# Gathering expert results after the last expert's weights, and an earlier silu-times-up product on VectorE

## The chip, the cores and the metric

The kernel runs on one core of a Trainium2 chip. The metric is the device time of one execution in microseconds (us); the kernel before took 1556.19 us, the median of three runs (1555.83 to 1558.44).

## What is computed

Two blocks on 512 tokens of width 1024, in float32. The first is two attention layers, and the second an attention and convolution layer followed by a mixture of experts and a last norm. Only the mixture and the last norm matter here:

```python
y_e = (silu(x_e @ w_gate[e]) * (x_e @ w_up[e])) @ w_down[e]   # for each of 32 experts, on its own rows
out[token] = x[token] + sum over the token's two experts of weight * y_e[row]   # gate folded in
out = rms_norm(out, g_final)
```

Each token picks two of the 32 experts. An expert has three weight matrices of 2048 KB each (gate, up, down), so the mixture streams 32 x 3 of them from memory.

## The kernel before, in words

The program is written by hand, one instruction stream for each engine, tied by semaphores. What an engine runs is in the order of its stream; nothing overtakes.

The mixture is a list of 32 items, one expert each, ordered by how many rows the expert has. SyncE issues the three weight loads of an item (`load_expert`, L602 to L610) into one of three sets of buffers (`it.p`), each when the item three places earlier has read its matrix; arrival is counted on `e_in[p][0..2]` (gate, up, down). All go through one queue, q1.

An item on TensorE (`item`, L1242) is: gate and up products (`gate_up`, L1191), then, when VectorE has multiplied silu(gate) by up (`swiglu`, L2462 to L2468), four or fewer transposes (L1263), and when ScalarE has copied these back (L1646), the down product (`down`, L1218). VectorE scales the result by the norm gate (`gated_results`, L2470 to L2484), and ScalarE stores it to the buffer `ys` in memory (`expert_results`, L1653), for all items but the last two.

The results of the first 30 items are brought to their tokens by GpSimd: it waits for every such store (`y_out`, L1767 and L1768), then issues eight indirect DMAs (L1772), two for each of the four token tiles `t`, of 128 rows of 4 KB each. `gath[t]` counts them. VectorE adds both to `x` in `add_results(t)` (L2498 to L2504).

The last two items (30 and 31), with few rows, aren't stored. TensorE multiplies their results by a selection matrix (`sums`, L1231 to L1240, with the matmuls of `sum_up` at L1227), eight banks for each item, and VectorE adds each bank to `x` (`add_sum`, L2492 to L2496). `sums(0)` stands ahead of item 31 on TensorE, `sums(1)` is its last work. After the experts each engine reads a word that says whether some expert had more rows than planned (L1280, L1659, L1775, L2551) and branches past a loop; here it has none to run. VectorE then makes the additions of `sums(1)`, ScalarE the squares of the last norm (L1665), GpSimd the reciprocal root (`rstd`, L1682 to L1692), VectorE the last product (L2572), and SyncE stores `out` (L651).

So the end of VectorE's stream before is: additions of `sums(0)`; `add_results(0)` and `(1)`; the product of silu and up for item 31; `add_results(2)` and `(3)`; the gated result of item 31; the read and branch; the additions of `sums(1)`.

Of the kernel before, what the change touches and what calls it, by code (L numbers as in the profile page):

```python
# [161 lines left out]
def fused_kernel(nc, a, out, xs, ys, table):  # L162

    with ExitStack() as ctx:
# [3 lines left out]
        def sem(name):  # L168
            return ctx.enter_context(nc.semaphore(name))
# [208 lines left out]
        e_in = [[sem(f"expert_{n}_loaded{p}") for n in ("gate", "up", "down")] for p in range(3)]  # L378
# [148 lines left out]
        items = plan.items  # L527
# [29 lines left out]
        def bank_of_sum(j):  # L557


            return psum[2 * (1 + j % 3) + late_pieces[0].bank] if j < SUMS else psum[j % 4]  # L560
# [1108 lines left out]
        def _(pool):  # L1669
# [97 lines left out]
            for n in range(5):  # L1767
                pool.wait_ge(y_out[n], 16 * (P // (NARROW if n > 2 else WIDE)) * plan.stores[n])  # L1768
            pool.sem_inc(pool_passed, 1)
            for t in range(TT):  # L1770
                for k in range(2):
                    gp.indirect_dma_start(gathered[k][:, t, :], None, ys[:, :],  # L1772
                                          bass.IndirectOffsetOnAxis(ap=dest[:, k, t:t + 1], axis=0)).then_inc(gath[t], 16)
# [13 lines left out]
        def _(dve):  # L1787
# [5 lines left out]
            def chain(ins):  # L1793
                steps(ins)
                steps.settle()
# [666 lines left out]
            def swiglu(it, unrolled=True):  # L2462
                for pc in it.pieces:
                    if not unrolled or pc.used:
                        dve.wait_ge(hT_done[pc.bank], pc.used)
                    dve.wait_ge(sg_ready[pc.bank], pc.used + 1)
                    v.tensor_tensor(h_act[pc.bank][:, 0:pc.ff], sg[pc.bank][:, 0:pc.ff], psum[2 + pc.bank][:, pc.ff:2 * pc.ff],  # L2467
                                    ALU.mult).then_inc(h_ready[pc.bank], 1)  # L2468

            def gated_results(it, unrolled=True):  # L2470


                for pc in it.pieces:
                    dve.wait_ge(down_done[pc.bank], pc.used + 1)
                    if unrolled and pc.stores:
                        dve.wait_ge(y_out[pc.buffer], 16 * pc.tiles_stored * pc.stores)
                    if pc.slots is None or pc.size == WIDE:
                        v.tensor_tensor(y_buf[pc.buffer][:, 0:pc.cols], psum[6 + pc.bank][:, 0:pc.cols], gates[pc.size], ALU.mult)\
                            .then_inc(y_ready[pc.bank], 1)
                        continue  # L2480
                    times = W // pc.cols
                    v.tensor_tensor(y_buf[pc.buffer].rearrange("p (c n) -> p c n", c=times),
                                    psum[6 + pc.bank][:, 0:pc.cols].unsqueeze(1).to_broadcast([P, times, pc.cols]),
                                    late_gate.rearrange("p (c n) -> p c n", c=times), ALU.mult).then_inc(y_ready[pc.bank], 1)  # L2484
# [7 lines left out]
            def add_sum(j, bank, done, taken, n):  # L2492

                t, cols = place_of_sum(j)
                dve.wait_ge(done, n + 1)
                v.tensor_tensor(x[:, t, cols], bank[:, :], x[:, t, cols], ALU.add).then_inc(taken, 1)  # L2496

            def add_results(t):  # L2498

                dve.wait_ge(gath[t], 32)  # L2500
                for k in range(2):
                    chain(v.scalar_tensor_tensor(out=x[:, t, :], in0=gathered[k][:, t, :], scalar=own_slot[:, k * TT + t, 3:4],
                                                 in1=x[:, t, :], op0=ALU.mult, op1=ALU.add))
                dve.sem_inc(results_added, 1)  # L2504
# [37 lines left out]
            for j in range(SUMS):  # L2542
                add_sum(j, bank_of_sum(j), summed_up, sum_taken, j)
            dve.wait_ge(sum_taken, SUMS)
            add_results(0)
            add_results(1)
            swiglu(items[-1])
            add_results(2)
            add_results(3)
            gated_results(items[-1])  # L2550
            n_pairs = dve.value_load(over_ids[0:1, OVER + 1:OVER + 2], min_val=0, max_val=OVER // 2)  # L2551
            with dve.If(n_pairs > 0):
                flip(further_items(0)[0], items[-1])
# [96 lines left out]
```

## Time and profile before

| | us |
|---|---|
| three runs | 1556.19 median, 1555.83 to 1558.44 |
| span of the profiled execution | 1554.6 |
| around that span, taken as the median less the span | 1.5 |
| TensorE busy | 1383.2 (89%) |
| VectorE busy | 698.1 (45%) |
| ScalarE busy | 356.0 (23%) |
| GpSimd busy | 112.0 (7%) |

The profile is of one execution. All times in it count from the start of its span. The change touches only the last 60 us of it, so the views of that stretch say what it is worth: the chain of work that ended last, the timelines of the engines, and the DMA queues. q1 holds the weight loads and the store of `out`, q10 the stores of expert results, q0 what GpSimd issues (the gathers, and before them the rows of each item), and q8 and q14 instructions. A "q" behind an engine's name marks work of its sequencer (waits, reads of a word, branches, DMA issues).

### The profile page before, as it was taken

What the parts mean: (1) busy time and instruction counts of PE and PEld (TensorE: products, weight loads), DVE (VectorE), ACT (ScalarE), POOL (GpSimd) and SP (SyncE); (2) the same over time, 40 slices, a digit from 0 to 9 for tenths busy, and PEclk for the clock granted to TensorE, in tenths of its full rate; (3) what the DMA queues carried; (4) which work ended last, traced back from release to release, by engine and by line L of the source; (5) the groups of instructions that cost most, each with busy time, mean ns of one, the idle gap of its engine ahead of it and who ended that gap; (6) DMA issues with size and microseconds to landing.
All of it is one profiled execution on the core that took longest, in us unless ns stands there. A gap on an engine that the chain in (4) does not pass through costs nothing.

```text
span 1554.6 us, 17575 instructions
## 1 busy us (share of the span) xinstructions
PE 1383.2 (89%) x6694; PEld 699.9 (45%) x6694; DVE 698.1 (45%) x1274; ACT 356.0 (23%) x778; POOL 112.0 (7%) x227
## 2 busy tenths in 40 slices
PE   4999999999999999999899978979996977869784
PEld 2444445554464445664644445455442333323341
DVE  4675515884366623322499775263121112111125
ACT  2433205562310344421400064110000000000001
POOL 3000000100100000002100000112000000000012
PEclk9999999999999999999899999989997989889996
DMA  9763136004376541003524123169999999999994
GB/s 340 268 243 109 54 108 129 1 1 162 100 259 211 188 162 55 1 0 109 165 81 161 54 109 151 66 247 391 421 416 418 422 419 416 425 420 426 421 401 168
DMA packets 85133, 338.08 MB, mean 217 GB/s; under 512 B 10343, under 2 KB 16280, under 8 KB 72376
## 3 DMA queue, kind: packets, MB, share of 16 engines
q1 hardware_dynamic: 70752, 307.24, 50.8%
q0 software_dynamic: 5664, 13.70, 3.1%
q10 hardware_dynamic: 8632, 15.99, 2.9%
q8 instruction: 55, 0.90, 0.2%
q14 instruction: 30, 0.25, 0.0%
HBM read 323.34 MB, written 17.24 MB: 219 GB/s over the span
## 4 chain that ended last, share of the span: by engine, by line
PE 68%; DMA 15%; DVE 11%; issue 3%; ACT 2%; POOL 1%; DVEq 0%; SPq 0%; ACTq 0%; POOLq 0%
PE score_banks L712 14%; PE bank L720 13%; DMA slots<-in_w_exp_up 11%; PE score_banks L1191 9%; PE bank L1218 5%; PE score_banks L720 4%; PE bank L928 3%; PE bank L696 3%; PE score_banks L1205 2%; PE bank L883 2%; PE bank L1030 2%; PE score_banks L1021 2%; DVE bufD L1982 2%; PE score_banks L940 1%; DMA slots<-in_w_mod 1%
## 5 line engine op out<-in xcount | busy, mean ns | idle before, releaser
L712 PE MATMUL score_banks<-slots 128*128 128x512 f32 (+1 forms) x584 | 246.0, 579 | 6.2 <-ACTq L1350 3.6
L720 PE MATMUL bank<-slots 128*128 128x512 f32 x480 | 209.4, 593 | 2.0 <-PE bank L720 0.9
L1191 PE MATMUL score_banks<-slots,norm_row 128*64 128x512 f32 (+1 forms) x672 | 151.5, 617 | 44.3 <-DMA slots<-in_w_exp_up 42.0
L712 PEld LDWEIGHTS score_banks<-slots 128*128 128x128 f32 x584 | 112.5, 195 | 132.9 <-issue 129.5
L2467 DVE TENSOR_TENSOR mix<-probsT,score_banks 128x256 f32<-128x256 f32 (+1 forms) x39 | 14.4, 370 | 285.3 <-ACT probsT L1641 285.1
L720 PEld LDWEIGHTS bank<-slots 128*128 128x128 f32 x480 | 89.9, 190 | 112.9 <-issue 111.7
L1218 PE MATMUL bank<-slots,mix 128*64 128x512 f32 (+1 forms) x864 | 118.3, 489 | 11.5 <-issue 9.5
L1641 ACT ACTIVATE probsT<-score_banks 128x256 f32<-128x256 f32 (+1 forms) x39 | 13.4, 343 | 441.7 <-PE score_banks L1191 381.2
L1191 PEld LDWEIGHTS score_banks<-slots,norm_row 128*64 128x64 f32 (+1 forms) x672 | 50.6, 144 | 139.1 <-issue 137.8
L720 PE MATMUL score_banks<-slots 128*128 128x512 f32 (+1 forms) x256 | 95.2, 527 | 0.3 <-PE score_banks L720 0.3
L2359 DVE SCALAR_TENSOR_TENSOR bufD<-slots,col,bufD 128x512 f32<-128x512 f32 x120 | 80.5, 750 | 0.4
L1218 PEld LDWEIGHTS bank<-slots,mix 128*64 128x64 f32 (+1 forms) x864 | 45.8, 124 | 68.1 <-issue 61.3
L1191 PE MATMUL score_banks<-slots,mix 128*32 128x256 f32 x896 | 57.2, 412 | 21.1 <-DMA slots<-in_w_exp_up 21.1
L1982 DVE SCALAR_TENSOR_TENSOR bufD<-slots,silu_c,bufD 128x512 f32<-128x512 f32 x91 | 68.4, 752 | 5.0 <-DMA slots<-in_w_mod 1.6
L2060 DVE TENSOR_TENSOR mix<-bank,gate_row 128x512 f32<-128x512 f32 x24 | 16.6, 692 | 112.9 <-PE bank L720 112.6
L720 PEld LDWEIGHTS score_banks<-slots 128*128 128x128 f32 x256 | 46.4, 190 | 44.1 <-issue 44.1
L928 PE MATMUL bank<-slots 128*128 128x512 f32 x128 | 61.8, 613 | 0.4 <-PE bank L883 0.4
L1682 POOL TENSOR_SCALAR pw<-ss 128x1 f32<-128x1 f32 (+3 forms) x25 | 7.1, 284 | 764.3 <-ACT slots L1338 411.9
L1736 POOL DMA_INDIRECT bufD<-normed_rows,w_router x30 | 30.5, 1016 | 411.1 <-PE score_banks L1180 387.0
L696 PE MATMUL bank<-k_sb,slots 128*128 128x128 f32 x312 | 45.4, 284 | 14.8 <-DVE slots L2425 9.4
L1982 DVE SCALAR_TENSOR_TENSOR slots<-slots,silu_c 128x512 f32<-128x512 f32 x70 | 52.6, 752 | 9.2 <-DMA slots<-in_w_mod 6.3
L1191 PEld LDWEIGHTS score_banks<-slots,mix 128*32 128x32 f32 x896 | 32.7, 118 | 50.6 <-issue 37.6
(358 smaller groups left out, 1722.8 us busy)
## 6 DMA issues: line engine op xcount, KB each, us to landing
slots<-in_w_exp_down SPq DMA_DIRECT2D x32, 2048.0 KB
slots<-in_w_exp_gate SPq DMA_DIRECT2D x32, 2048.0 KB, 28.8
slots<-in_w_exp_up SPq DMA_DIRECT2D x32, 2048.0 KB, 33.6
slots<-in_w_in SPq DMA_DIRECT2D x16, 2048.0 KB, 8.8
slots<-in_w_mod SPq DMA_DIRECT2D x24, 1024.0 KB, 5.2
slots<-in_ada_w SPq DMA_DIRECT2D x18, 1024.0 KB, 6.7
slots<-in_w_out SPq DMA_DIRECT2D x6, 2048.0 KB, 7.8
slots<-in_ada_w SPq DMA_DIRECT2D x3, 2048.0 KB, 20.3
```

The costliest lines, as they stand in the source:

```text
L696: last = nc.tensor.transpose(bank[:, i * P:(i + 1) * P], piece, ident)
L712: last = mm(bank[:, cols], w[:, k, lo:lo + P], src[:, k, cols], start=(k == 0), stop=(k == kts - 1))
L720: last = mm(bank[:, 0:cols], src[:, k, t * P:(t + 1) * P], rhs(k), start=(k == 0), stop=(k == kts - 1))
L883: last = mm(psum[banks][r][:, :], rows[:, k, r * P:(r + 1) * P], weights[:, k, :], start=(k == 0), stop=(k == 3))
L928: ins = mm(gate_bank(group)[:, :], hT[:, k, t * P:(t + 1) * P], z_units[u][:, k, :], start=(k == 0), stop=(k == KT - 1))
L1021: mm(bank[:, :], hT[:, 2 * pair + c, t * P:(t + 1) * P], A8[:, 2 * pair + c, :], start=True, stop=False)
L1030: last = mm(bank[:, c * P:(c + 1) * P], pT[:, j * P:(j + 1) * P], C_tok[:, j, h * P:(h + 1) * P], start=(j == 0), stop=(j == TT - 1))
L1191: last = mm(out, rows[:, k, :], e_gu[it.p][:, :, k, c * pc.ff:(c + 1) * pc.ff], start=(k == 0), stop=(k == KT - 1))
L1205: last = mm(psum[2 + pc.bank][c * pc.size:(c + 1) * pc.size, m * pc.ff:(m + 1) * pc.ff], rows[:, k, :], e_gu[it.p][:, m, k, c * pc.ff:(c + ...
L1218: last = mm(psum[6 + pc.bank][c * pc.size:(c + 1) * pc.size, 0:pc.cols], hTe[pc.bank][:, lo:lo + pc.size], e_down[it.p][:, f, c * pc.cols: ...
L1982: return v.scalar_tensor_tensor(out=acc, in0=w, scalar=c, in1=acc, op0=ALU.mult, op1=ALU.add)
L2359: conv_at[j] = steps(v.scalar_tensor_tensor(out=conv[:, j, :], in0=src, scalar=wcol, in1=conv[:, j, :], op0=ALU.mult, op1=ALU.add))
```

## The change

GpSimd waits, ahead of its eight gathers, for the down weights of the last item. VectorE makes the last item's product of silu and up ahead of `add_results(0)`, and its gated result between `add_results(1)` and `(2)`.

```diff
@@ gpsimd, L1767 @@
             for n in range(5):
                 pool.wait_ge(y_out[n], 16 * (P // (NARROW if n > 2 else WIDE)) * plan.stores[n])
             pool.sem_inc(pool_passed, 1)
+            pool.wait_ge(e_in[items[-1].p][2], 16 * items[-1].loads)
             for t in range(TT):
                 for k in range(2):
                     gp.indirect_dma_start(gathered[k][:, t, :], None, ys[:, :],
@@ vector, L2542 @@
             for j in range(SUMS):
                 add_sum(j, bank_of_sum(j), summed_up, sum_taken, j)
             dve.wait_ge(sum_taken, SUMS)
+            swiglu(items[-1])
             add_results(0)
             add_results(1)
-            swiglu(items[-1])
+            gated_results(items[-1])
             add_results(2)
             add_results(3)
-            gated_results(items[-1])
             n_pairs = dve.value_load(over_ids[0:1, OVER + 1:OVER + 2], min_val=0, max_val=OVER // 2)
```

## Rows read from the trace of the kernel before

**Rows 1.** The page: TensorE clock, DMA busy share and rate in 40 slices.
```profile
PEclk9999999999999999999899999989997989889996
DMA  9763136004376541003524123169999999999994
GB/s 340 268 243 109 54 108 129 1 1 162 100 259 211 188 162 55 1 0 109 165 81 161 54 109 151 66 247 391 421 416 418 422 419 416 425 420 426 421 401 168
```

**Rows 2.** The chain that ended last: start us, us, what.
```profile
1499.66 10.68 DMA expert_results<-bufD
...
1510.36 0.02 POOLq L1768
...
1510.64 0.76 issue
1511.40 0.97 POOL slots L1772
...
1515.16 11.47 DMA slots<-expert_results,dest
...
1530.72 3.64 PE bank L1218 x32
1534.36 1.70 issue
```

**Rows 3.** Timeline of VectorE: start us, us, engine, line, operation, count, idle before.
```profile
1523.82 2.60 DVE L2502 SCALAR_TENSOR_TENSOR x<-slots,sums,x 128x1024 f32<-128x1024 f32 x2 [6.70 <-DMA slots<-expert_results,dest]
...
1529.69 5.35 DVE L2502 SCALAR_TENSOR_TENSOR x<-slots,sums,x 128x1024 f32<-128x1024 f32 x4
1535.27 0.69 DVE L2482 TENSOR_TENSOR bufD<-bank,slots 128x512 f32<-128x512 f32 x1 [0.22 <-DVE x L2502]
1538.14 1.29 DVE L2496 TENSOR_TENSOR x<-score_banks,x 128x512 f32<-128x512 f32 x2 [2.18 <-PE score_banks L1227]
1539.85 4.16 DVE L2496 TENSOR_TENSOR x<-score_banks,x 128x512 f32<-128x512 f32 x6 [0.42 <-PE score_banks L1227]
```

**Rows 4.** Timeline of SyncE: the issues of item 31's gate and down weights.
```profile
1482.49 0.34 SPq L610 DMA_DIRECT2D slots<-in_w_exp_gate  x1
...
1485.81 0.33 SPq L610 DMA_DIRECT2D slots<-in_w_exp_down  x1
```

**Rows 5.** DMA issues from 1482.4 to 1483.5: KB each, us to landing.
```profile
slots<-in_w_exp_gate SPq DMA_DIRECT2D x1, 2048.0 KB, 28.8
```

**Rows 6.** DMA queues in 1510:1512, 1518:1520, 1520:1522, 1522:1524: packets, MB, share.
```profile
q1 hardware_dynamic: 38, 0.52, 61.3%
...
q1 hardware_dynamic: 18, 0.23, 26.9%
...
q1 hardware_dynamic: 4, 0.03, 3.9%
...
q0 software_dynamic: 216, 0.80, 98.3%
```

**Rows 7.** Stretches: busy us (count) by engine, granted clock, DMA share, GB/s.
```profile
1490.00:1495.00 5.00, 4.08 (x26) 1.72 (x24) 1.25 (x4) 0.77 (x2) 0.00 (x0) 1.00 1.01 426
...
1526.00:1528.00 2.00, 0.00 (x0) 0.00 (x0) 1.72 (x3) 0.00 (x0) 0.00 (x0) 0.50 0.45 184
1528.00:1530.00 2.00, 0.17 (x1) 0.17 (x1) 1.78 (x3) 0.00 (x0) 0.00 (x0) 0.50 0.25 102
```

**Rows 8.** Timeline of GpSimd: the first two and the last of the eight gathers.
```profile
1511.40 0.97 POOL L1772 DMA_INDIRECT slots<-expert_results,dest  x1 [26.17 <-issue]
1512.67 0.95 POOL L1772 DMA_INDIRECT slots<-expert_results,dest  x1 [0.30 <-issue]
...
1520.14 0.94 POOL L1772 DMA_INDIRECT slots<-expert_results,dest  x1 [0.30 <-issue]
```

**Rows 9.** Line 1772, all eight gathers, from issue to landing.
```profile
DMA to landing us min/median/max: 6.9/9.2/11.5
```

**Rows 10.** DMA issues, whole span: the store of the output.
```profile
out<-slots SPq DMA_DIRECT2D x4, 512.0 KB, 2.7
```

**Rows 11.** Line 2551 on VectorE's sequencer: ns min/median/max.
```profile
L2551 DVEq TENSOR_LOAD <-inv_sums x1: 546/546/546, 1535.3 to 1535.3; - x1
```

**Rows 12.** Timeline of TensorE and ScalarE: item 31's gate and up, its silu.
```profile
1516.62 2.86 PE L1191 MATMUL score_banks<-slots,norm_row 128*32 128x256 f32 x44 [0.24 <-issue]
...
1524.47 0.28 ACT L1641 ACTIVATE probsT<-score_banks 128x128 f32<-128x128 f32 x1 [16.51 <-PE score_banks L1191]
```

## The prediction

> **What bounds the kernel now.** I read the page's 40 slices first. From the slice at about 1050 us on, the DMA engines are full and move some 420 GB/s until the last two slices [rows 1]: the mixture runs at the rate of its weights. The change doesn't touch that rate. It touches what comes after the weights, so the next view is the chain of work that ended last. It goes from the last store of expert results, which lands 10.68 us after its issue, to GpSimd's wait at 1510.36, to the gathers, and stays with a gather until 1526.64 [rows 2]. From there VectorE adds the gathered rows and makes item 31's product, TensorE multiplies by the down weights (3.64 us) and sums, and VectorE adds the sums.
>
> The timeline of VectorE shows how tight this end is. It has nothing from 1517 until the first pair of gathers is in at 1523.8, then four `add_results` with little idle time up to 1535.04 (5.35 us from 1529.69), the gated result until 1535.96, then 2.18 us idle while TensorE sums, and the eight additions from 1538.14 to 1544.01 [rows 3]. What follows is the norm and the output store, which the change leaves as they are. So the number to forecast is when the last addition ends, now 1544.01.
>
> Last, the DMA queues. The down weights of item 31 are issued at 1485.81, behind gate and up [rows 4]. Gate, issued at 1482.49, lands 28.8 us later [rows 5], at 1511.3. q1 still moves 0.52 MB in 1510 to 1512, 0.23 MB in 1518 to 1520 and 0.03 MB in 1520 to 1522 [rows 6]. The last weights are thus in at about 1521 to 1522, 10 us after GpSimd began to gather. While gathers and weights run together the DMA share isn't full at first (q1 61.3% in 1510 to 1512, when hardly a gather moves yet), and at the end it falls to 0.45 and 0.25 with gathers left [rows 6, 7]. The 16 engines reach their ends at different times: some have had their weights long before, and those that had weights until 1521 finish the gathers last.
>
> **The change, part by part.** *GpSimd's new wait.* It lets the gathers start only when the down weights are in. I need that time without gathers beside it. From 1511.3 two loads of 2.097 MB (up and down) are left for the engine that is last; at the 426 GB/s of the full stretch [rows 7] one takes 4.92 us, so 1521.2. Gate and up and down share the engines with gathers now, and some of those 9.9 us may shrink as other engines fall idle. The lower bound comes from q1's packets being large (0.52 MB in 38) and the gathers' small (0.80 MB in 216) [rows 6]: if both queues take turns by packet, 3.7 KB of gather stand beside 13.7 KB of weights, a fifth of the engine's time in 1513 to 1521.5, or 1.8 us, and the weights would be in at 1519.7 rather than 1521.5. I take 1520.8, near the row of the full stretch, with 1519.7 and 1521.8 as ends.
>
> Behind the waiting instruction on GpSimd's queue stand the eight gathers, its own read and branch, and the reciprocal roots of the last norm, which wait for VectorE's last additions in any case. From the last wait to the first gather it takes 1.04 us (1510.36 to 1511.40, 0.76 us of it preparation) [rows 2]; three of the waits that are now in it are then past, so I take 0.95. A gather is issued every 1.25 us (1511.40 and 1512.67, 1520.14 for the eighth) [rows 8]. First issue 1521.75, second 1523.0, eighth 1530.5.
>
> *How long a gather takes with no weights beside it* is what the trace doesn't show. Eight of them took 6.9 to 11.5 us to landing, all in a crowd [rows 9]; that is the upper side. The lower side is 0.94 us in which GpSimd writes the descriptors [rows 8] and the 2.7 us that a 512 KB store of `out` takes on idle engines [rows 10]: 3.6 us. The second waits up to 1.25 us for the first, which is as large. I take 4.5, nearer to the idle case because nothing else is queued. So the first pair is in at 1527.5 (now 1523.8), the last at 1535.0 by the issues, and hardly sooner by the bytes: 4.19 MB at 410 GB/s are 10.2 us.
>
> The Trainium skill gives this price in DMA: Bandwidth & Descriptors, "Anatomy of one DMA": 2.0 us and the bytes at 436 GB/s, an estimate of 3.2 us for 512 KB, or 4.1 with the writing of descriptors. No run here shows it. By it, the end would come some 0.4 to 1.3 us sooner than with my 4.5.
>
> *VectorE's order.* `add_results` costs 2.75 us to the next one (1529.69 to 1535.04 is two of them, 5.35) [rows 3], so four are 10.95 us with their waits, and the gated result between them adds 0.69 and about 0.1. From 1527.6 that is 11.7 us: 1539.3. The last pair of gathers, in at 1535.0, would allow an end at 1537.7, so the adding is the bound, by 1.6 us. Item 31's product of silu and up is moved ahead of it all. Its cover: silu is done at 1524.75 now, and gate and up begin at 1516.62 [rows 12]; both are before 1527.5, so the product (0.29 us), the transposes, the copy and the down product (3.64 us at the clock of 0.50 that rows 7 show) end before 1530, beside VectorE's wait and additions. That takes item 31's product and down product off the chain. The gated result then has its input when its turn comes, at about 1533.2, and TensorE's first four sums (3.8 us) are ready at about 1538, before VectorE wants them.
>
> *What this uncovers.* Now the gated result is VectorE's last work ahead of the branch, and the read of the word and the branch lie in the 2.18 us in which it waits for the sums. After the change they stand open behind `add_results(3)`. The read is 0.55 us [rows 11], with the register work and the branch 0.97 us from 1535.29 to 1536.26; what the first instruction past the branch costs isn't seen. Bounds: 1.0 us, and the 2.85 us from 1535.29 to 1538.14, at which the sums came in. I take 1.6. So the eight additions start at 1540.9. Six of them take 4.16 us back to back [rows 3], eight 5.6. TensorE refills a bank in 0.95 us at the low clock while VectorE takes 0.7, and with four filled ahead that still is enough.
>
> *Sum.* 1520.8 + 0.95 + 1.25 + 4.5 + 0.1 + 11.7 + 1.6 + 5.6 = 1546.5, against 1544.01: 2.5 us later. Of it, the start of the first pair is 3.7 later, the chain of VectorE behind it from the first gather to the last addition is 18.9 us against 20.2 now. To the median, 1556.2 + 2.5 = 1558.7.
>
> **The rivals.**
> 1. *The wait is longer than it seems (slower).* The pair lands as in a crowd: all 16 engines gather at once from one memory, no longer some early and some late. At the row's least, 6.9 us [rows 9], the end is 2.4 us later than in the sum: +4.9, 1561.1. With weights at 1521.8 as well, +5.9, 1562.1. It decides from 5.1 us on, where the total loss passes 3.1 us. For it: each of the eight rows. Against it: the engines were loaded in all of them.
> 2. *The reordering is worth more than the delay.* Weights at 1519.7, a pair in 3.6 us, 1.0 for the branch: 2.6 us less than the sum, so -0.1, 1556.1. To be faster by over 3.1 us, even with these low ends, the weights would have to be in at 1516.7, when at the full rate the up weights alone are due (1511.3 + 4.9 = 1516.2); this takes engines that speed up greatly once others are idle.
> 3. *The wait doesn't bind.* If, in most executions, the down weights are in before the stores, only the new order counts. VectorE ends `add_results(3)` at 1535.1 or up to 0.5 later for the gated result between, reads and branches by 1537.2, and ends at 1542.8: -1.2, 1555.0. q1's bytes until 1522 speak against it [rows 6].
>
> The Trainium skill, DMA: Bandwidth & Descriptors, "Queues, rings and completion order", says that each DMA engine takes its queues in turn, a packet at a time. Here the 128 KB store beside the weights took 10.68 us, in agreement with a shared engine. The rule speaks for the change as far as the weights go, and it is the lower end of 1519.7 above; it doesn't turn the sign, since the gathers' bytes must be moved behind the weights all the same.
>
> **How the numbers follow.** About 0.2% (3.1 us) is what a measurement of this kernel can tell from no change. The forecast, a loss of 0 to 3.1 us: 0.50. Rival 1, with other ways to lose more: 0.35. Rival 2: 0.08, a third of it faster by over 0.2%. Rival 3: 0.05, all within 0.2%. Faster by something that isn't in the trace: 0.02. So faster 0.05, same 0.60, slower 0.35. The range from 1555.0 (rival 3) to 1562.1 (rival 1 at its upper end) leaves out 2 in 10. Most of the cases inside are above the time before, so a loss that can hardly be measured is what I expect.
>
> **What would show it.** In the changed kernel's profile, GpSimd's first gather at 1521 to 1523 and none before the last weights; DMA nearly idle for 2 to 3 us between them; landings within 5 us of issue; VectorE's first gathered addition at 1527 to 1528; the down product of item 31 well before that; and the eight additions starting 1.0 to 2.0 us after `add_results(3)` with no idle time between. I am wrong if the weights are in before 1519 or after 1523, if gathers land under 3.6 us or over 6, or if the branch shows no cost.

## The result and the profile after

The changed kernel took 1562.31 us (median of 8 runs, 1559.62 to 1565.85) against 1557.3 us for the kernel before (8 runs, 1555.54 to 1558.44): the ratio is 1.0036, with an interval from 1.0027 to 1.0045. It is slower by 5.0 us in the medians (5.6 by the ratio), more than the 3.1 us that were called the limit of what can be told. A second comparison gave 1.0025 (1.0011 to 1.0039).

The profiled execution has a span of 1559.7 us, 5.1 more than before. First the timeline of GpSimd in the changed kernel (start us, us, engine, line, operation, idle time before it), which answers to [rows 8]:

```profile
1523.24 0.96 POOL L1773 DMA_INDIRECT slots<-expert_results,dest  x1 [36.78 <-DMA slots<-in_w_exp_down]
1524.51 0.95 POOL L1773 DMA_INDIRECT slots<-expert_results,dest  x1 [0.31 <-issue]
...
1532.71 1.01 POOL L1773 DMA_INDIRECT slots<-expert_results,dest  x1 [0.30 <-issue]
```

The gathers wait for the down weights, and start 11.8 us later than before. The stretches of the same kernel (busy us of TensorE, its weight load, VectorE, ScalarE and GpSimd, then granted clock, DMA share, GB/s) show what that leaves on the DMA engines:

```profile
1510.00:1512.00 2.00, 1.92 (x32) 1.08 (x32) 0.08 (x2) 0.00 (x0) 0.00 (x0) 1.00 0.65 279
...
1518.00:1520.00 2.00, 1.96 (x33) 1.26 (x36) 1.04 (x2) 0.00 (x0) 0.00 (x0) 1.00 0.23 98
1520.00:1522.00 2.00, 2.00 (x40) 1.13 (x31) 0.00 (x0) 0.00 (x0) 0.00 (x0) 1.00 0.11 41
1522.00:1524.00 2.00, 0.78 (x13) 0.48 (x13) 0.29 (x1) 0.56 (x2) 0.76 (x1) 1.00 0.00 0
1524.00:1526.00 2.00, 1.50 (x28) 0.78 (x20) 0.00 (x0) 0.00 (x0) 1.39 (x3) 1.00 0.40 66
1526.00:1528.00 2.00, 0.00 (x0) 0.00 (x0) 0.00 (x0) 0.00 (x0) 1.64 (x2) 1.00 0.98 385
```

In 1510 to 1512 the share of busy DMA engines has begun to fall. In 1518 to 1522 the DMA share is 0.23 and 0.11: most of the 16 DMA engines have had their weights and stand still, where in the kernel before they gathered. From 1522 to about 1525 all of them stand still. Then VectorE's timeline, which answers to [rows 3]:

```profile
1522.49 0.29 DVE L2468 TENSOR_TENSOR mix<-probsT,score_banks 128x128 f32<-128x128 f32 x1 [3.44 <-ACT probsT L1641]
1530.31 5.35 DVE L2503 SCALAR_TENSOR_TENSOR x<-slots,sums,x 128x1024 f32<-128x1024 f32 x4 [7.53 <-DMA slots<-expert_results,dest]
1535.88 0.69 DVE L2483 TENSOR_TENSOR bufD<-bank,slots 128x512 f32<-128x512 f32 x1 [0.22 <-DVE x L2503]
1536.49 5.35 DVE L2503 SCALAR_TENSOR_TENSOR x<-slots,sums,x 128x1024 f32<-128x1024 f32 x4
1543.46 4.15 DVE L2497 TENSOR_TENSOR x<-score_banks,x 128x512 f32<-128x512 f32 x6 [1.62 <-issue]
1547.91 1.29 DVE L2497 TENSOR_TENSOR x<-score_banks,x 128x512 f32<-128x512 f32 x2 [0.30 <-PE score_banks L1227]
```

The product of silu and up is out of the way, VectorE waits 7.53 us for the first pair of gathers, and from 1530.31 on it hardly stops until the last addition ends at 1549.20, 5.2 us later than 1544.01. The branch stands open with 1.62 us. The down product of item 31, which before ran at 1530.72 in 3.64 us at a granted clock of 0.50 (1.2 GHz) [rows 2, 7], follows the gate and up products closely and takes 1.93 us, at 1.00 (2.4 GHz):

```profile
1518.36 3.66 PE L1191 MATMUL score_banks<-slots,norm_row 128*32 128x256 f32 x64
1522.83 0.33 PE L1263 MATMUL bank<-k_sb,mix 128*128 128x128 f32 x1 [0.81 <-DVE mix L2468]
1523.57 1.93 PE L1218 MATMUL bank<-slots,mix 128*32 128x256 f32 x32 [0.41 <-issue]
1536.67 3.78 PE L1227 MATMUL score_banks<-bufD,sinT 64*128 64x512 f32 x8 [11.17 <-DVE bufD L2483]
```

That gain is real and lies beside VectorE's wait, where it is worth nothing.

### The profile page after: what moved, and what is told of

Its sections match the earlier page's. It is cut to its first block, busy times and chain, and to the rows that moved or that the text cites. A ratio compares the mean times of both kernels' runs of the same rounds, so it can differ in the third digit from the quotient of the medians.

```text
span 1559.7 us, 17574 instructions
## 1 busy us (share of the span) xinstructions
PE 1380.8 (89%) x6694; PEld 703.8 (45%) x6694; DVE 698.3 (45%) x1274; ACT 356.2 (23%) x778; POOL 112.3 (7%) x227
## 4 chain that ended last, share of the span: by engine, by line
PE 63%; DMA 17%; DVE 14%; issue 3%; ACT 2%; POOL 1%; SPq 0%; DVEq 0%; POOLq 0%; ACTq 0%
DMA slots<-in_w_exp_up 13%; PE bank L720 12%; PE score_banks L712 10%; PE score_banks L1191 8%; DVE bufD L2360 5%; PE score_banks L720 5%; PE bank L1218 4%; PE bank L696 3%; PE bank L928 3%; PE score_banks L1205 2%; PE bank L883 2%; PE bank L1030 2%; PE score_banks L1021 2%; DMA slots<-in_ada_w 2%; DVE bufD L1983 2%
## 5 line engine op out<-in xcount | busy, mean ns | idle before, releaser
L1191 PE MATMUL score_banks<-slots,mix 128*32 128x256 f32 x896 | 54.6, 399 | 19.3 <-DMA slots<-in_w_exp_up 19.3
L696 PEld LDWEIGHTS bank<-k_sb,slots 128*128 128x128 f32 x312 | 35.8, 147 | 38.8 <-DVE slots L2426 16.8
## 6 DMA issues: line engine op xcount, KB each, us to landing
slots<-in_w_exp_down SPq DMA_DIRECT2D x32, 2048.0 KB, 36.3
slots<-in_w_exp_gate SPq DMA_DIRECT2D x32, 2048.0 KB, 29.5
slots<-in_ada_w SPq DMA_DIRECT2D x3, 2048.0 KB, 20.5
```

The lines of the kernel that those rows point to most:

```text
L696: last = nc.tensor.transpose(bank[:, i * P:(i + 1) * P], piece, ident)
L1191: last = mm(out, rows[:, k, :], e_gu[it.p][:, :, k, c * pc.ff:(c + 1) * pc.ff], start=(k == 0), stop=(k == KT - 1))
```

## The experiments

Three theories were set against each other. *A:* the loss is the late start of the gathers. *B:* VectorE's new order costs it (the insertion between the additions, and the open branch). *C:* the weight stream of the changed program is itself later, and little of the loss is the wait's.

**How the profiles are compared.** The mixture before the end doesn't take the same time in each execution. So I count from one event, G: the landing of item 31's gate weights on the last of the DMA engines. It is the issue in SyncE's timeline and the time to landing in the DMA issues. In the kernel before 1482.49 + 28.8 = 1511.3 [rows 4, 5]; in the changed one 1483.73 + 29.5 = 1513.2, and its down weights are in at 1487.04 + 35.9 = 1522.9:

```profile
1483.73 0.34 SPq L610 DMA_DIRECT2D slots<-in_w_exp_gate  x1
1487.04 0.33 SPq L610 DMA_DIRECT2D slots<-in_w_exp_down  x1
slots<-in_w_exp_gate SPq DMA_DIRECT2D x1, 2048.0 KB, 29.5
slots<-in_w_exp_down SPq DMA_DIRECT2D x1, 2048.0 KB, 35.9
```

All columns but G are us after G, good to 0.1. The pair is in when VectorE's first addition of it starts. The last pair's landing is the last issue and its time to landing; that of the down weights their issue and theirs, which the first profile of before doesn't give (q1 has one packet, of 0.00 MB, left in 1522 to 1524 there).

| kernel | G | first gather | down weights | first pair | last pair | last addition |
|---|---|---|---|---|---|---|
| before | 1511.3 | 0.1 | | 12.5 | 20.3 | 32.7 |
| before, again | 1512.2 | 0.5 | 12.2 | 13.6 | 21.0 | 32.5 |
| new order, no wait | 1514.2 | -0.5 | 11.4 | 12.4 | 19.8 | 31.3 |
| spread order, no wait | 1512.0 | 0.7 | 11.1 | 13.1 | 20.6 | 31.6 |
| waits for up | 1513.1 | 5.1 | 9.9 | 12.3 | 20.5 | 31.3 |
| waits for up, early read | 1509.9 | 5.1 | 9.9 | 13.0 | 20.5 | 31.4 |
| the same, again | 1514.2 | 5.1 | 10.0 | 12.3 | 21.0 | 30.8 |
| the change | 1513.2 | 10.0 | 9.7 | 17.1 | 24.9 | 36.0 |
| the change, again | 1510.5 | 10.1 | 9.8 | 17.0 | 25.0 | 36.3 |
| wait alone, old order | 1511.8 | 10.0 | 9.7 | 16.5 | 25.3 | 37.4 |

**The new order alone.** In the changed kernel:

```diff
-            pool.wait_ge(e_in[items[-1].p][2], 16 * items[-1].loads)
```

> The new order on VectorE alone, GpSimd's gathers start as in the kernel before. Theory A (the loss of 5 us is the gathers' late start): between -0.6 and +0.5 us against the kernel before. VectorE waits for silu until 1524.75 instead of starting on gathered rows at 1523.8 (+1.0), has the gated result in between (+0.5), opens the branch (+1.6), and loses the 2.2 us of waiting for the sums. Theory B (the new order costs it): +3 us or more. Theory C (the changed program's weight stream is itself some 2 us later): about +2 us, with the last stores landing near 1512 instead of 1510.4.

Measured: 1557.03 us (12 runs), ratio 1.0003 (0.9994 to 1.0011). B falls. In time the order neither costs nor gives anything that shows; after G it is even 1.3 us shorter than before (31.3 against 32.6, the mean of the two profiles of before), since its TensorE work is ready in time. Its timeline of VectorE has both effects in it, 1.62 us at the branch and no wait for the down product:

```profile
1525.52 0.29 DVE L2467 TENSOR_TENSOR mix<-probsT,score_banks 128x128 f32<-128x128 f32 x1 [7.19 <-ACT probsT L1641]
1526.66 5.36 DVE L2502 SCALAR_TENSOR_TENSOR x<-slots,sums,x 128x1024 f32<-128x1024 f32 x4 [0.85 <-DMA slots<-expert_results,dest]
...
1539.81 4.16 DVE L2496 TENSOR_TENSOR x<-score_banks,x 128x512 f32<-128x512 f32 x6 [1.62 <-issue]
```

**The wait alone.** In the kernel before:

```diff
             pool.sem_inc(pool_passed, 1)
+            pool.wait_ge(e_in[items[-1].p][2], 16 * items[-1].loads)
```

> GpSimd's wait for the down weights alone, with VectorE's old order. Theory A: slower than the changed kernel by 1 us, so +6 us against before: the first two additions end at 1535.7 as in the changed kernel, then product, transposes, copy and down product end at about 1541, gated result 1542, first sum 1544.3, last addition 1550.2. Theory B: about +2 us. Theory C: +2 us more than what the gathers' start says, in both.

Measured: 1562.7 us (6 runs), ratio 1.0045 (1.0031 to 1.0059), +7.0 us by the ratio and 5.5 in the medians. The whole loss is in the wait, and after G the new order wins back 1 us or so of it: last addition at G + 37.4, against 36.0 and 36.3. The times of the two kernels can't be told apart, their intervals overlap.

**A wait for the up weights.** In the changed kernel:

```diff
-            pool.wait_ge(e_in[items[-1].p][2], 16 * items[-1].loads)
+            pool.wait_ge(e_in[items[-1].p][1], 16 * items[-1].loads)
```

> The changed kernel, but GpSimd waits for the last item's up weights instead of its down weights, which land 4.9 us earlier (1518.1 against 1523.0 in the changed kernel). Theory A, if each us of delay counts in full: +0 to +1 us against before. If instead the DMA engine that is last with its weights sets the end of the gathers, the gathers end only when that engine has done its down weights and 10 us of gathers: the gain over the changed kernel is then about 3 us, the empty time of that engine, so +2 us. Theory B: as slow as the changed kernel, +5 us.

Measured: 1555.68 us (12 runs), ratio 0.9993 (0.9983 to 1.0003). This run says most. GpSimd's first gather in it:

```profile
1518.24 0.96 POOL L1773 DMA_INDIRECT slots<-expert_results,dest  x1 [30.28 <-DMA slots<-in_w_exp_up]
```

and VectorE's first additions of gathered rows:

```profile
1525.39 5.36 DVE L2503 SCALAR_TENSOR_TENSOR x<-slots,sums,x 128x1024 f32<-128x1024 f32 x4 [2.75 <-DMA slots<-expert_results,dest]
```

The first gather is issued at 1518.24, that is G + 5.1, 5 us later than without a wait, and still the first pair is in at G + 12.3 and the last at G + 20.5, as without it (12.4 to 13.6, and 19.8 to 21.0). With the wait for down the issues are 4.9 us later again, and the pairs 4.7 and 4.4 us later. So a start at G + 5 is still free, and from there to G + 10 each us costs close to one. No start between the two was run; since a us of delay can't cost much more than one, nearly all of the 4.9 us must count, and the turn lies close to G + 5. The second of my expectations under A, that such a start would still cost 2 us, was wrong. Without a wait, what lands the gathers is the DMA engine that is last with its weights, whenever they were issued. The profile doesn't name single engines; that few are left at the end is read from the DMA share, 0.45 and then 0.25 in the kernel before [rows 7]. An estimate agrees: from G on, at 426 GB/s [rows 7], that engine has its share of two loads to move (9.8 us) and its share of eight gathers (4.19 MB, 9.8 us), which makes the first pair G + 12.3 and the last G + 19.7 at the earliest. Measured with starts up to G + 5.1 are 12.3 to 13.6 and 19.8 to 21.0. With the start at G + 5.1, GpSimd's issues reach G + 14.7, the last pair is in 5.9 us later, and the two limits meet. With the start at G + 10 the issues and the time to landing are the limit alone.

**Before and after, again.** Both kernels unchanged.

> The kernel before, unchanged, as a control of the comparison and for a second profiled execution. Counted from the landing of the last item's gate weights on the slowest DMA engine (G), the first profile had the first pair of gathers in at G + 12.4, the last at G + 20.3 and the last addition at G + 32.7 us. Theory A, in the form that the first runs leave (gathers may start up to about 5 us after G at no cost, and each us beyond costs one): the same three figures within 1 us, and 0 us in the comparison. Theory C: G itself lies within 1 us of the first profile's 1511.3. If G moves by 1 to 3 us between executions of one kernel, the 1.9 us of the changed kernel are chance and C falls.

> The changed kernel, unchanged, again beside the kernel before. Theory A: first gather issued at G + 10.0, first pair in at G + 17, last at G + 25, last addition at G + 36, so 3 to 4 us behind the kernel before in these terms, and +3 to +5.6 us in time. Theory C: G at 1513 or later again, and the time stays 2 us above what the last addition's distance from G gives.

Measured: before against before 1.0001 (0.9992 to 1.001), the change 1.0025 (1.0011 to 1.0039), +3.9 us. After G the figures of the changed kernel repeat within 0.3 us. Those of before repeat less well: last addition 32.7 and 32.5, but first pair 12.5 and 13.6, last pair 20.3 and 21.0. G itself doesn't repeat: 1510.5 here for the changed kernel, 1513.2 in the first profile, and 1509.9 to 1514.2 over all ten, with no order by kernel. C falls as the reason of those 1.9 us: the first profile of the change was behind at G by chance, and of the 5.1 us between the two spans some 3.3 are the change. What the time still has above that is taken up under the prediction.

**Another order without a wait.** In the kernel before:

```diff
             add_results(0)
-            add_results(1)
             swiglu(items[-1])
+            add_results(1)
             add_results(2)
-            add_results(3)
             gated_results(items[-1])
             n_pairs = dve.value_load(...)
+            add_results(3)
```

> No wait. VectorE makes the product of silu and up between add_results 0 and 1, the gated result between 2 and 3, and reads the word for the branch ahead of add_results 3. Theory A: faster than before by 1.0 to 2.0 us: the down product (3.6 us at the low clock) ends at 1531.7, the gated result at 1533.3, add_results 3 at 1536.1, the branch at 1536.8 and the eight additions at 1542.5, against 1544.0. Theory B: no gain or a loss, since each insertion delays the gathered additions. Theory C says nothing on it.

Measured: 1555.83 us (12 runs), ratio 0.9997 (0.9987 to 1.0008). After G the last addition is 1.0 us sooner than before, the low end of what was expected, and the time can't tell it from none.

**An early read.** In the kernel that waits for up:

```diff
             gated_results(items[-1])
+            n_pairs = dve.value_load(...)
             add_results(2)
             add_results(3)
-            n_pairs = dve.value_load(...)
```

> GpSimd waits for the last item's up weights, VectorE has the changed order, and the read of the word for the branch stands behind the gated result, ahead of add_results 2. Theory A: the read (0.9 us open behind add_results 3 in the changed kernel) lies beside the gated result; idle time between add_results 3 and the additions 0.7 instead of 1.62 us, and 0.9 us less than with the up wait alone, so 1.0 to 2.5 us faster than before. Theory B: no difference from the kernel with the up wait.

> The kernel with the up wait and the read ahead of add_results 2, a second time, to narrow the interval of its first comparison (0.9994, from 0.9985 to 1.0003). Theory A: the last addition at G + 30.5 to 31.5, against G + 32.5 to 32.7 in the two profiles of the kernel before, so 1 to 2 us or 0.06 to 0.13% faster than before.

Measured: 1553.73 us (11 runs), ratio 0.9994 (0.9985 to 1.0003), and in the second comparison 1556.26 us (12 runs), 0.9991 (0.9982 to 1.0000). VectorE's timeline in the second:

```profile
1533.02 5.36 DVE L2503 SCALAR_TENSOR_TENSOR x<-slots,sums,x 128x1024 f32<-128x1024 f32 x4 [0.23 <-issue]
1539.10 4.16 DVE L2497 TENSOR_TENSOR x<-score_banks,x 128x512 f32<-128x512 f32 x6 [0.73 <-DVE x L2503]
```

The gap at the branch is 0.73 us instead of 1.62, and 0.23 opens at the read: 0.7 us net. This is the best found of the kernels that give the right result. Both comparisons lean to a gain of about 1 us over the kernel before, and after G the last addition is 1.1 to 1.9 us sooner (31.4 and 30.8); it is under what one comparison can tell.

**Half the bytes.** The sum had 4.5 us from the second issue to the first pair, measured were 5.8 and 5.6 us. To see whether the bytes are the reason, each gather was cut to 64 rows, with the wait and, leaving its line out too, without it. The other 64 tokens of each tile get what was in the buffer.

```diff
-                    gp.indirect_dma_start(gathered[k][:, t, :], None, ys[:, :],
-                                          bass.IndirectOffsetOnAxis(ap=dest[:, k, t:t + 1], axis=0)).then_inc(gath[t], 16)
+                    gp.indirect_dma_start(gathered[k][0:64, t, :], None, ys[:, :],
+                                          bass.IndirectOffsetOnAxis(ap=dest[0:64, k, t:t + 1], axis=0)).then_inc(gath[t], 16)
```

> The changed kernel, but each gather brings 64 rows of 4 KB instead of 128; the other 64 tokens of each tile get what was in the buffer. Eight issues and the same waits stay, half the bytes go. In the changed kernel the first pair was in 5.8 us after the second issue, where 4.5 was forecast. If the bytes of both make up the difference: 4.2 to 4.6 us, first pair 1.4 us sooner, and the time 1.2 us or so less than the changed kernel's. If it is a fixed cost of such a DMA: 5.5 us or more, and no gain.

> The new order on VectorE without GpSimd's wait, and gathers of 64 rows instead of 128 (the other 64 tokens of each tile get what was in the buffer). Theory A says that without the wait the gathers end when the DMA engine that is last has moved its weights and then its share of gathered bytes: with half the bytes the last pair is in at about G + 15.5 to 17 instead of G + 20 to 21 (G: landing of the last item's gate weights), the first pair at G + 11 to 12. If instead GpSimd's issues set it, the last pair would stay 11 us behind the last issue. The down weights land at G + 10 to 10.8, between the 11.1 to 12.3 with full gathers beside them and the 9.8 with none. Time: 0 to 2.5 us under the kernel with the new order alone.

Measured: with the wait 1558.78 us (10 runs), ratio 1.0025 (1.0014 to 1.0036), first pair 5.2 us after the second issue. That is between the 4.2 to 4.6 and the 5.5 that would have decided, and the ratio is that of the changed kernel with full gathers: inconclusive. Without the wait 1568.62 us (4 runs), ratio 1.0066 (1.0051 to 1.0082), some 10 us slower than before with half the bytes, which none of the theories expected. Its stretches:

```profile
1515.00:1520.00 5.00, 2.04 (x7) 0.59 (x4) 2.75 (x5) 0.00 (x0) 3.61 (x4) 0.87 1.03 159
1520.00:1525.00 5.00, 0.00 (x0) 0.00 (x0) 0.00 (x0) 0.00 (x0) 1.80 (x2) 0.50 1.01 150
```

The DMA engines are busy throughout and move 150 GB/s, and the down weights land 50.9 us after their issue, where the kernels with full gathers and no wait have 36.1 to 36.7. So the edit had changed two things, the bytes and the partitions written. The next two keep all 128 partitions and halve the rows to 2 KB; they aren't the right halves, and the other half of each token's sum is what was in the buffer:

```diff
-                    gp.indirect_dma_start(gathered[k][:, t, :], None, ys[:, :],
+                    gp.indirect_dma_start(gathered[k][:, t, 0:W], None, ys.rearrange("r (h n) -> (r h) n", h=2),
```

> The changed kernel, but each gather brings 128 rows of 2 KB instead of 4 KB (halves of rows, not the right ones; the other half of each token's sum is what was in the buffer). The run with 64 rows changed a second thing: it wrote to half of the partitions, and moved 190 to 240 GB/s where the full gathers move 330 to 385. With all partitions in use and half the bytes, if bytes make up the difference to the forecast of 4.5 us: first pair in 4.6 us or less after the second issue (5.2 to 5.8 us with full rows), last pair 4.5 us or less after the last issue. If it is a fixed cost of such a DMA: 5.2 us or more for the first pair.

> The same gathers of 2 KB rows without GpSimd's wait, VectorE in the new order. The 64-row gathers beside the weights were 10 us slower, with the down weights in at G + 25 instead of G + 11.4 (G: landing of the last item's gate weights). If that came from writing to half of the partitions, the 2 KB rows don't show it: down weights in at G + 10 to 11, first pair at G + 11 to 12.5, last at G + 14 to 17 (the DMA engine that is last has half the gathered bytes left after its weights), and the time is at or up to 2.5 us under the kernel with the new order alone. If any gather of smaller pieces beside weights has this effect, the time is 5 us or more over it.

Measured with the wait (a single run, so the time says little): 1557.3 us against a median of 1557.28 for before. The time of the eight gathers from issue to landing is, in the changed kernel:

```profile
DMA to landing us min/median/max: 4.7/5.8/6.1
```

and in the kernel with half rows:

```profile
DMA to landing us min/median/max: 3.6/3.7/4.5
```

The first pair is in 4.5 us after the second issue. So the bytes make up the difference to the forecast, as far as one profile can say: 4.5 us is what a pair of half the size takes. The three profiles of full rows have 5.8, 5.6 and 5.2, so the step to the lowest of them, 0.7 us, is little more than their own spread. Without the wait: 1554.25 us (10 runs), ratio 0.9984 (0.9974 to 0.9994), down weights at G + 10.9, first pair at G + 11.1, last pair at G + 16.0, last addition at G + 30.1. The gathers' last landing moves 4 to 5 us forward with half of the 10 us of bytes, while GpSimd issues as ever: without a wait they are bound by the bytes of the last DMA engine, as A has it. The estimate above gives G + 11.1 and G + 14.8 for the two pairs here. The slow case didn't come back, so it isn't made by fewer bytes or smaller pieces. It goes with the form of 64 rows on 64 partitions; which of the two, the count of rows or the partitions, makes it wasn't separated.

## Why the prediction was wrong

The mechanism was right, and what was forecast as "no change that can be told" was a loss that can: 0.60 stood on within 0.2%, 0.35 on slower. The measured 1562.31 lies 0.2 us above the range. The signs listed came, later by the 1.9 us of G, but for the landings (4.7 to 6.1 us, not within 5) and what hangs on them, VectorE's first gathered addition at 1530.31. Term by term, in us after G of each profile (the forecast took G as 1511.3):

- *Weights in.* Forecast G + 9.5 (1520.8), measured 9.7 and 9.8. Two loads at the full rate, 1521.2 or G + 9.9, was the right estimate; I had gone below it for a gain from engines left alone, and none came. That gathers slow the weights is so: 11.1 to 12.2 in the three profiles without a wait that give it, 9.7 to 10.0 in the six with one. So the change does bring the weights 1.3 to 2.5 us sooner. The Trainium skill's rule that each DMA engine takes its queues in turn, a packet at a time (DMA: Bandwidth & Descriptors, "Queues, rings and completion order"), gave 1.8; by that rule, the traces agree on the difference. The forecast took it off the wrong figure: with gathers beside them the weights are in at G + 11.1 to 12.2 and not at G + 10.2 (1521.5), so the end 1519.7 was 1.3 us too low.
- *From the wait to the first gather.* Forecast 0.95, measured 0.2 to 0.3. The preparation of 0.76 us falls into the new wait. 0.7 too much.
- *The pair's time to landing.* Forecast 4.5, measured 5.8, 5.6, and 5.2 with the old order. This is the step that failed, a term mis-sized by 1.2 us. It was built from an idle store and one transfer ahead; the half-row run, with 4.5, suggests that the figure fits half the bytes. The Trainium skill's price for a gather (DMA: Bandwidth & Descriptors, "Anatomy of one DMA"), 3.2 us, is lower still: no gather of 512 KB landed under 4.6 us in the two profiles of the changed kernel, and half rows of 256 KB took 3.6 us at least where the page's sum gives 2.6. The 4.1 of the forecast puts GpSimd's 0.94 us on top, though the page counts the writing of descriptors in its 2.0. The measured times decide.
- *How times to landing are to be read.* Both gathers of a pair count on one semaphore, `gath[t]`, and the view takes the first half of the pair's arrivals for the first gather. So its figure for a first gather is only a lower bound, and that for a second is the pair's. In the second profile of before the eight alternate, 6.0 to 6.8 and 11.7. [rows 9] has figures for only two of its eight gathers, 6.9 and 11.5; the 6.9, on which the first rival was priced, is such a bound and no landing of a gather.
- *VectorE from the first pair to the last addition.* Forecast 18.9 (11.7, 1.6 and 5.6), measured 18.9 (1530.31 to 1549.20) in the first profile, with each part within 0.2, and 19.3 in the second, where VectorE waited 0.46 us for the second pair. The forecast had no wait there.
- *The kernel before.* Its last addition is at G + 32.7 and 32.5, as read.

Together: the forecast had the last addition at G + 35.2, the runs have it at 36.0 and 36.3; the loss by structure is 3.5 us where 2.5 were forecast. That alone puts it past the 3.1 us. Of the 3.6 us between the forecast time, 1558.7, and the measured 1562.3, this is 1.0. Another 1.1 is level: the three runs shown of before had a median of 1556.2, all eight 1557.3, and the forecast was built on the first. The other 1.5 stays open. Both comparisons show such a rest, of 2.1 and 0.4 us: they give +5.6 and +3.9 us, with intervals from 1.7 to 7.0 together, and the first one's lower end, 4.2, is above 3.5. The kernel with the wait alone shows it too (+7.0 by the ratio, 4.8 after G). No run says where it arises.

Of the rivals, the first (the pair lands late) was the case in kind, in part: its point of decision was put at 5.1 us, the landings took 5.2 to 5.8. Its reason, that all 16 engines gather at once, was tested by no run, and its other half, weights at 1521.8 (G + 10.5), didn't come. The second didn't occur: the DMA engine that is last didn't speed up when others fell idle. Two loads took 9.7 to 10.0 us after G in each kernel with a wait, against 9.84 at the rate of the full stretch. The third was excluded by GpSimd's idle row, which ends with the down weights. But its price, -1.2 us for the order alone, was about right after G (-1.3), though the time shows none of it.

One thing the prediction had no step for: the start of the gathers isn't what bound them before. It priced the delay from the landing (1523.8 to 1527.5) and got its size about right, but it didn't ask from which start on a delay begins to count. That point, close to G + 5, is what the wait for up shows.

## What to carry to other kernels

In this kernel, a transfer that shares the DMA engines with the last loads is bound by the engine that finishes those loads last. It can be issued later at no cost, up to the point where issue time and landing time alone reach that engine's end, and beyond it each us counts. So a wait that keeps two transfers apart is better set on an earlier load than the last. Here even that gave nothing that can be told in time (0.9993), since its gain (the weights, here 1.3 to 2.5 us sooner) is worth something only if those weights are what the end waits for. When profiles of single executions are compared for a few us, count from a common event near the end: here the stream ahead of it moved by 4.3 us between executions, more than the change did.

## What the runs showed of the hardware

- Gathers of 64 rows on 64 of 128 partitions, beside weight loads, held both up: 150 GB/s together with the DMA share at 1.0, and the last weights 14 us later. Half rows on all partitions, with the same bytes, didn't. Alone, the two forms can't be told apart by rate: 186 to 236 GB/s in 1524 to 1530 with the wait, and 168 to 221 in 1524 to 1532 for half rows. Both are near what GpSimd issues, 262 KB each 1.21 to 1.25 us, or 210 to 217 GB/s, so the 328 to 385 GB/s of full gathers, with twice the bytes for each issue, say nothing against them. The low rate named in the expectation for half rows is thus no sign of the partitions. From 1526 to 1528, with 64 rows and with half rows:

```profile
1526.00:1528.00 2.00, 0.00 (x0) 0.00 (x0) 1.44 (x2) 0.00 (x0) 1.54 (x2) 0.62 0.89 236
1526.00:1528.00 2.00, 0.00 (x0) 0.00 (x0) 1.74 (x2) 0.00 (x0) 1.70 (x2) 0.94 0.78 221
```

- The DMA engines' ends are far apart. In the changed kernel the DMA share falls to 0.65 in 1510 to 1512 already, with the last down weights in at 1523; the fast engines had theirs over 10 us before.
- Issuing a gather took longer once VectorE's additions ran. Before, all eight took 0.94 to 0.97 us; in the changed kernel the seventh, issued at 1530.73 just after VectorE had begun at 1530.31, took 1.67. Each full-gather kernel with a wait has one such gather, of 1.15 to 1.82 us. That VectorE is the reason is a reading of these times and was tested by no run:

```profile
1530.73 1.67 POOL L1773 DMA_INDIRECT slots<-expert_results,dest  x1 [0.30 <-issue]
```
